# The memory's opening: first weight chunk loaded and rounded ahead of the memory, its squares behind the second chunk

## The reference, cut to what matters

```python
def memory_cross_attention(xn, memn, wq, wk, wv, wo, q_norm, k_norm):
    q = rms_normalize((xn @ wq).reshape(B, S, XA_HEADS, XA_HEAD)) * q_norm
    k = rms_normalize((memn @ wk).reshape(B, M, XA_HEADS, XA_HEAD)) * k_norm
    v = (memn @ wv).reshape(B, M, XA_HEADS, XA_HEAD)
    ...                       # softmax(q k^T / 16) v, then @ wo
memn = rmsnorm(mem, mem_norm_g)   # mem * rsqrt(mean(mem^2) + eps) * g
```

## Time and profile before

| quantity | value |
|---|---|
| median of 3 runs | 1319.56 us (1319.38 to 1319.75) |
| the profiled execution, its own time | 1318.44 us |
| its span | 1316.6 us |
| PE busy | 1269.6 us (96%) |
| DVE / ACT / POOL busy | 638.0 / 543.6 / 538.7 us |
| chain that ended last | PE 86%, DVE 8%, ACT 4%, issue 2% |

### The profile page before, as it was taken

The page is one execution under the profiler, slowest core; times in us unless marked ns, Lnnn a source line. Parts: engine busy times, 40 slices in busy tenths (PEclk is TensorE's granted clock), DMA queues, the critical chain, the costliest instruction groups (busy, mean ns, idle before and its releaser), DMA issues.

```text
span 1316.6 us, 19858 instructions
## 1 busy us (share of the span) xinstructions
PE 1269.6 (96%) x8194; PEld 1007.3 (77%) x8194; DVE 638.0 (48%) x995; ACT 543.6 (41%) x834; POOL 538.7 (41%) x432
## 2 busy tenths in 40 slices
PE   6999999999999999999999899999999999999999
PEld 5778887766768888766787667778788888888887
DVE  4450002886440166696448647265565656562000
ACT  5541434676665233463544444353422323221111
POOL 6554443131333454364142126421455555544443
PEclk9999999999999999999999999999999999999999
DMA  9835221202112222421220023300222222222223
GB/s 391 331 138 194 97 96 65 81 33 81 64 65 91 87 88 91 186 87 64 80 91 5 3 82 120 150 33 32 96 96 97 96 96 96 96 76 88 88 88 108
DMA packets 20549, 133.26 MB, mean 101 GB/s; under 512 B 2280, under 2 KB 2408, under 8 KB 7408
## 3 DMA queue, kind: packets, MB, share of 16 engines
q1 hardware_dynamic: 18720, 119.50, 25.4%
q10 hardware_dynamic: 1744, 12.53, 2.5%
HBM read 125.71 MB, written 6.31 MB: 100 GB/s over the span
## 4 chain that ended last, share of the span: by engine, by line
PE 86%; DVE 8%; ACT 4%; issue 2%; DMA 0%; POOL 0%; SPq 0%; ACTq 0%; DVEq 0%
PE banks L425 84%; PE banks L432 2%; DVE arena L2005 1%; DVE arena L1859 1%; ACT arena L1141 1%; DVE arena L1969 1%; DVE arena L2004 0%; ACT arena L1310 0%; ACT arena L1309 0%; DMA arena<-in_mem 0%; DVE arena L1812 0%; DVE arena L1856 0%; ACT arena L1311 0%; DVE arena L2031 0%; DVE arena L2030 0%
## 5 line engine op out<-in xcount | busy, mean ns | idle before, releaser
L2301 POOL TENSOR_TENSOR weights_low<-weights,weights_high 128x512 fp32r<-128x512 f32 (+1 forms) x388 | 498.5, 1316 | 669.7 <-ACT weights_high L1104 669.7
L425 PE MATMUL banks<-h_high_low,weights_high 128*128 128x512 f32 x880 | 356.0, 405 | 2.4 <-POOL weights_low L2301 1.3
L425 PE MATMUL banks<-h_high_low,weights_low 128*128 128x512 f32 x880 | 347.6, 395 | 0.0
L425 PE MATMUL banks<-h_low,weights_high 128*128 128x512 f32 x880 | 347.5, 395 | 0.0
L1104 ACT ACTIVATE weights_high<-weights 128x2048 fp32r<-128x2048 f32 (+2 forms) x105 | 178.2, 1697 | 343.4 <-PE banks L425 331.0
L425 PEld LDWEIGHTS banks<-h_high_low,weights_high 128*128 128x128 f32 x880 | 165.2, 188 | 48.4 <-issue 7.1
L425 PEld LDWEIGHTS banks<-h_low,weights_high 128*128 128x128 f32 x880 | 165.2, 188 | 41.0 <-issue 2.9
L425 PEld LDWEIGHTS banks<-h_high_low,weights_low 128*128 128x128 f32 x880 | 164.9, 187 | 40.4
L425 PE MATMUL banks<-arena 64*64 64x64 f32 (+4 forms) x1288 | 104.8, 280 | 15.1 <-DVE arena L1812 6.4
L425 PEld LDWEIGHTS banks<-arena 64*64 64x64 f32 (+3 forms) x1288 | 73.8, 152 | 37.4 <-issue 17.9
L1939 DVE TENSOR_TENSOR xres<-banks,xres 128x512 f32<-128x512 f32 x24 | 16.6, 690 | 141.2 <-PE banks L425 141.2
(11 more groups left out here) (347 smaller groups left out, 2045.6 us busy)
## 6 DMA issues: line engine op xcount, KB each, us to landing
weights<-in_stream SPq DMA_DIRECT2D x83, 1024.0 KB, 4.9
weights<-in_down SPq DMA_DIRECT2D x16, 704.0 KB, 4.0
arena<-in_ada SPq DMA_DIRECT2D x8, 1024.0 KB, 12.3
arena<-in_ada SPq DMA_DIRECT2D x8, 512.0 KB, 7.3
h<-in_stream SPq DMA_DIRECT2D x2, 1024.0 KB, 9.1
xres<-in_x SPq DMA_DIRECT2D x1, 2048.0 KB, 28.5
x_kept<-xres ACTq DMA_DIRECT2D x1, 2048.0 KB, 6.3
xres<-x_kept ACTq DMA_DIRECT2D x1, 2048.0 KB, 7.8
```

What stands on the lines that cost most here:

```text
L425: ins = nc.tensor.matmul(o, lhsT, rhs, start=start, stop=stop, skip_group_check=skip)
L2301: nc.gpsimd.tensor_tensor(lo_of(c)[:, cols], raw_of(c)[:, cols], hi_of(c)[:, cols].bitcast(F32), ALU.subtract).then_inc(sem("weights_split ...
```

## The change

Five orders are changed, and no arithmetic.

- SP: chunk 0 is loaded ahead of the memory, chunk 1 ahead of the constants, and x ahead of the third and fourth ada loads.
- ACT: chunk 0 is rounded (four pieces) ahead of the memory's eight high parts, chunk 1 right behind them. Then come two squares, chunk 2 in one instruction, and the other six squares. Before, four squares stood between chunks 0 and 1, four behind chunk 1, and chunk 2 behind all.
- PE: `norm_sum(0)` stands behind the third key tile, not behind the second.
- That sum goes to bank 5, alone in the ring for the moment; the ring goes on with 3, 0, 1, 2.
- POOL's and DVE's orders stay as they are.

```diff
@@ block.tensor
             project("kx", 2, KD, mem, MEM, lambda k: pe.wait_ge(sem("memory_ready"), k + 1))
+            project("kx", 1, KD, mem, MEM, first=2)
             pe.wait_ge(sem("consts_loaded"), 16)
+            M.use([5])
             norm_sum(0, MEM)
+            M.use([3, 0, 1, 2])
+            project("kx", 1, KD, mem, MEM, first=3)
             for c in range(1, 4):
-                project("kx", 2, KD, mem, MEM, first=2 * c)
+                if c > 1:
+                    project("kx", 2, KD, mem, MEM, first=2 * c)
@@ block.scalar
             act.wait_ge(sem("params_loaded"), 16)
+            for part in range(PIECES):
+                split_weights(part, PIECES)
             act.wait_ge(sem("mem_loaded"), 16)
             for k in range(KD):
                 nc.scalar.activation(memn_hi[:, k, :], mem_raw[:, k, :], ACT.Identity, scale=par("mem_g", k))\
                     .then_inc(sem("memory_hi"), 1)
             for part in range(PIECES):
                 split_weights(part, PIECES)
-            squares(0, mem_raw, MEM, lambda k: None, tiles_=range(4))
-            for part in range(PIECES):
-                split_weights(part, PIECES)
-            squares(0, mem_raw, MEM, lambda k: None, tiles_=range(4, KD))
+            squares(0, mem_raw, MEM, lambda k: None, tiles_=range(2))
             split_weights()
+            squares(0, mem_raw, MEM, lambda k: None, tiles_=range(2, KD))
@@ block.sync
-            sp.dma_start(mem_raw, mem_in).then_inc(sem("mem_loaded"), 16)
...
             chunk_in(0)
+            sp.dma_start(mem_raw, mem_in).then_inc(sem("mem_loaded"), 16)
+            chunk_in(1)
             sp.dma_start(consts[:, :], consts_in[:, 0:MIX_COL]).then_inc(sem("consts_loaded"), 16)
-            chunk_in(1)
...
             chunk_in(4)
+            sp.dma_start(xres[:, :, :], x_in).then_inc(sem("x_loaded"), 16)
             ada_in_(2)
             ada_in_(3)
-            sp.dma_start(xres[:, :, :], x_in).then_inc(sem("x_loaded"), 16)
```

## The result

The changed kernel takes 1325.55 us, median of 15 runs (1320.68 to 1329.15), beside 1320.69 for the kernel before in runs of the same time (15 runs, 1319.38 to 1322.74). The ratio is 1.0035, 95% interval [1.0026, 1.0044]: 4.9 us between the medians, 4.6 by the ratio. Forecast were 1323.8 and a step of +4.2; the 1323.8 stood on 1319.56 for the kernel before, which in these fifteen runs is 1320.69. The profiled execution took 1322.77, its span is 1320.9. All ratios compare fast executions alone, which leaves out one execution of b1_warm (1565.67 us at a mean granted clock of 0.753).

What follows compares the result with a forecast made beforehand. Bound: a single-file opening, then PE without slack. The 1.5 us paper gain becomes +4.2 through DVE and POOL alternating, other edits nothing: 1318.44 to 1322.6 profiled, median 1.1 above that execution, so 1323.8; range 1318.0 to 1326.6.

Steps and rivals of the forecast that it cites:

- likeliest case: Opening: DVE's low parts of the memory alternate with POOL's pieces, PE's clock high afterwards; +4.2 us, 1323.8, chance 0.42.
- The loads: Start of the load queue: chunk 0 takes the memory's place and lands at 6.94 us, the memory at 9.47.
- The turns: Opening: DVE's low parts 1.43 us apart, in turn with POOL's pieces, the last done about 20.8; first key tile +4.2 us.
- a memory 0.3 us earlier: Opening: low part 0 would slip in front of POOL's third piece, and the loss would be 0.4 us less.
- The clock: PE's opening: the first key tile's last three matmuls, behind the last low part, run at the higher clock, ending at 21.25.
- rival 1: Second key tile: PE's clock stays low through the trickle, some 20 matmuls 0.21 us apart; +6.2 us, 1325.8, chance 0.18.
- rival 2: Opening: DVE's low parts are starved, most waiting until chunk 2's last POOL piece at 23.4; +9.2 us, 1328.8, chance 0.12.
- rival 3: Opening: DVE's low parts stay 0.40 us apart, all moves up 1.5 us; 1318.1, chance 0.10 (mild form 0.15).
- Squares: Ahead of norm_sum: all squares added by 25 us, PE reaches the sum at 26.8; hidden by 1.8 us.
- side remark: norm_sum: left behind the second key tile (24.0 us), the sum would have cost about 1 us.
- x and the ada loads: Load queue: two ada loads land some 5 us later but are wanted past 44 us; costs nothing.
- The way to the end: PE between 12.3 and 20 us: any shift moves the end by the same amount, since nothing behind has slack.

Runs made afterwards that it cites:

- b1_warm: The kernel before with 16 dummy matmuls on PE ahead of the first key tile; ratio to the kernel before 0.9987.
- e2_x_back: The changed kernel with the load of x back behind the third and fourth ada loads; ratio to the kernel before 1.0034.
- a2_dve0: The changed kernel with chunk 0's four low parts on DVE ahead of the memory's, POOL beginning with chunk 1; 1317.94 us, ratio to the kernel before 0.9989.
- a1_psum: The changed kernel with the second input of DVE's eight low parts a zeroed PSUM bank (results wrong, same work); ratio to the kernel before 0.9977.
- e1_half: The changed kernel with POOL's instructions halved to 128x256 for chunks 0 and 1; ratio to the kernel before 0.9998.
- a0_again: The changed kernel run once more with no edit; 1325.45 us, ratio to the kernel before 1.0044.
- a3_warm: The changed kernel with 11 dummy matmuls on PE ahead of the first key tile; ratio to the kernel before 1.0026.
- a4_norm: The changed kernel with norm_sum back behind the second key tile, still in bank 5; ratio to the kernel before 1.0041.

## Why the prediction was right

The mechanism of the forecast's likeliest case, seven low parts each behind one POOL piece, is what the traces show. The closeness of the number is in part luck: two errors, -0.7 for the low parts and +1.2 for the clock, went opposite ways. Taken from 1320.69 instead of 1319.56, the forecast of +4.2 would have read 1324.9, and the 1322.5 to 1324.4 that the likeliest case gave itself 1323.6 to 1325.5; 1325.55 lies above the first and at the edge of the second.

**The loads.** Forecast: chunk 0 at 6.94, the memory at 9.47. Measured: chunk 0 in 5.3 us from its issue at 1.20, the memory in 7.29 from 1.67, so 6.5 and 8.96. Half a microsecond early, both of them. Single executions differ by more: where chunk 0 comes first, it lands between 6.16 (e2_x_back) and 7.39 (a2_dve0).

**The turns.** This was the term of +4.2. The rate, read off L1807, was right: forecast 1.43 apart and up to about 1.5 us long, measured 1.42 and 1544 ns. Low part 0 started at 9.64, 0.1 us ahead of POOL's third piece, and ran free, where the forecast had it just behind; so PE opened at 10.27 and not near 11.8. The prediction had named that case, for a memory 0.3 us earlier. But none slipped into the gap between POOL's chunks, which was 0.2 us instead of 0.8: one was ready at about 12.9, just when POOL began chunk 1. So seven met a piece, as many as forecast, though not the same seven. The last was done at 20.11, forecast 20.8. a1_psum shows the cause by taking it away, and e1_half shows the size of the price. The Trainium skill's "SBUF — State Buffer", section "Who interferes with whom", says that a DVE instruction with two SBUF inputs contends with a GpSimd instruction that reads SBUF. The traces agree, and add the rate: 1.42 us per low part instead of 0.40.

**The clock.** Here a term was mis-sized. The forecast took the higher level for everything behind the last low part and gave the lower one to rival 1. It was the lower one: 12 matmuls from 20.17 to 22.7 ran 0.21 apart instead of 0.115, 1.2 us. So rival 1 came true in its mechanism, with 12 such matmuls and 1.2 us where it had 20 and 2. In a0_again the lower level lasted to 24.9. a3_warm shows the trickle itself at 1.2 GHz, after a rise that the dummies had bought. So +4.60 at key tile 6 is the forecast's 4.2, less 0.7 for the low parts, plus 1.2 for the clock, within 0.1.

**Starvation (rival 2)** did not come for the low parts in any of the traces. The key tiles' own addition, 9.69 us before, is in the changed kernel:

```profile
31.48 1.00 DVE L1769 TENSOR_TENSOR arena<-arena 128x256 f32<-128x256 f32 x1 [0.33 <-ACT arena L1191]
```

One turn, beside a POOL run. The prediction held against this rival that the long wait was one case. It was not: b1_warm, which also has the order of before, has it again.

```profile
25.96 10.03 DVE L1766 TENSOR_TENSOR arena<-arena 128x256 f32<-128x256 f32 x1
```

In the other eleven traces no instruction of this line takes more than 1.29 us in the opening. What decides between one piece and eight stays open.

**No meeting (rival 3)** was ruled out by the trace; its price was right in sign. Without the meeting the change is worth 3 us by a1_psum, where the prediction had 1.5.

**The other edits.** Squares: DVE's adds ended at 24.1, forecast 25, and PE reached the sum at 27.27, forecast 26.8; the cover was there. The side remark that the sum behind the second tile would have cost 1 us was wrong (a4_norm): with the clock low, that tile ended at 24.5, behind the adds. x and the ada loads: nothing, as forecast (e2_x_back). Small slips of the sum change nothing: by its own steps low part 2 would be done at 13.6, not 13.8, and starvation is +9.1, not +9.2.

**The way to the end.** The prediction took every shift of PE in the opening to reach the end in full. In these traces it does so only roughly: +4.60 at key tile 6 was +3.26 at 668 us and +4.39 from 779 us on.

What is not settled is the spread of the whole times. It was 8.5 us over the 15 runs of the changed kernel beside 3.4 before, but later sets of the kernel before spread as much: 9.1 us over 24 runs. So it is not shown to belong to the change. The low parts lie alike in the five traces that have the changed kernel's helpers as they are. The moment of the clock's rise differs by 2 us, and the larger part arises between 668 and 779 us.

## What to carry to other kernels

When work is moved forward, look at which engine is then busy beside which, not only at what waits for what: in these traces DVE and POOL took turns, and a DVE instruction with two SBUF inputs that met POOL's work waited through one POOL instruction (in two traces one waited through eight). The price can be read off any place in the old trace where the same pair of forms already meets. It went away when one input came from PSUM or when DVE took the early pieces itself. With POOL's instructions halved, what a turn adds fell from 1.02 to 0.47 us.

Work that reaches TensorE in small portions did not raise its clock here: the close work behind it still began at the lower level (12 matmuls, 1.2 us), and a clock raised beforehand was lost (a3_warm). A forecast should price the first close matmuls at that level.

## What the runs showed of the hardware

- The profile's granted clock has nothing before its first change and then reads 1.00: in the changed kernel PE's starts are 0.21 us apart until 22.7, and a window there shows 1.00 (window, length, PE busy (x), PEclk, DMA share, GB/s). Only the starts tell.

```profile
13.10:20.50 7.40, 5.28 (x16) 1.00 1.01 426
```

- One scalar_tensor_tensor of 128x256 takes 473 ns with the second input in PSUM and 476 with both in SBUF, alone; beside POOL it takes 479 at most with the PSUM input, and up to 1544 with both in SBUF.
- Dummy matmuls raised the clock (at 6.2 us in a3_warm), but it fell again at 13.0, 2.9 us after the work had begun to trickle.
